# Where 128 w_ada accumulations stand in a one-core diffusion-layer kernel, and decay sums made from high and low parts

## What is computed

```python
sh1, sc1, g1, sh2, sc2, g2 = split(silu(c) @ w_ada + b_ada, 6)   # w_ada: 2048 x 12288
hx = rmsnorm(x) * (1 + sc1) + sh1                                # context: the same with c_ctx
z  = hx @ w_in             # q, k, v, two low-rank columns for decay, g, Hyena inputs, merge gates
la = log_sigmoid(lr @ wg + bg) / 16           # log decay of each direction, 256 x 512
# context: state = sum over tokens of k * exp(b_last - b) and v, with b = cumsum(la)
# latent:  chunked gated linear attention (chunks of 64) in both directions, FFT long convolution
x  = x + g1 * rmsnorm((sigmoid(ga) * (o @ p_gla) + sigmoid(gb) * (y @ p_hy)) @ w_out)
x  = x + g2 * rmsnorm(swiglu(rmsnorm(x) * (1 + sc2) + sh2))
```

## Time and profile before

| | |
|---|---|
| median of 3 runs | 1619.79 us |
| profiled execution, its own time | 1624.13 us |
| span of that execution | 1622.3 us |
| TensorE, busy share of the span | 98% |
| VectorE, ScalarE, GpSimd | 68%, 46%, 5% |
| mean granted TensorE clock | 0.991 |

### The profile page before, as it was taken

How to read it: one execution, slowest core, us unless ns; L and a number is a source line. 1 busy time by engine, 2 the same in 40 slices (tenths; PEclk the granted TensorE clock), 3 DMA queues, 4 the chain that set the end, 5 groups by cost and what they waited for, 6 DMA issues and landing times.

```text
span 1622.3 us, 22565 instructions
## 1 busy us (share of the span) xinstructions
PE 1593.1 (98%) x8540; PEld 1310.5 (81%) x8540; DVE 1102.0 (68%) x1325; ACT 751.6 (46%) x902; POOL 81.6 (5%) x157
## 2 busy tenths in 40 slices
PE   6999999999999999999999999999999999999998
PEld 4656678888888888888788888888888888888886
DVE  5668675788789868778776666666665556555556
ACT  5433225634544434444345545555445554444444
POOL 0011020000000001100100000000000000000000
PEclk9999999999999999999998999999999999999999
DMA  9999877766677768966984777777776656656653
GB/s 343 322 325 357 284 242 217 212 191 195 204 212 236 235 209 281 310 213 213 334 270 169 229 231 237 237 231 237 238 231 200 190 186 206 195 193 194 194 193 118
DMA packets 264785, 377.74 MB, mean 233 GB/s; under 512 B 14177, under 2 KB 223436, under 8 KB 263180
## 3 DMA queue, kind: packets, MB, share of 16 engines
q1 hardware_dynamic: 243008, 297.57, 58.3%
q0 software_dynamic: 20816, 78.91, 14.7%
q10 hardware_dynamic: 892, 0.33, 0.1%
HBM read 372.57 MB, written 4.19 MB: 232 GB/s over the span
## 4 chain that ended last, share of the span: by engine, by line
PE 92%; DMA 3%; DVE 2%; SPq 1%; issue 1%; ACT 0%; DVEq 0%; ACTq 0%
PE ps L1713 39%; PE ps L1720 19%; PE ps L1728 9%; PE ps L1729 8%; PE ps L1730 8%; PE ps L1655 2%; DMA a2raw<-in_w_ada 1%; SPq L438 1%; DMA ada_raw<-in_w_ada 1%; DVE lo L1152 1%; PE ps L1852 1%; PE ps L1864 0%; PE ps L1643 0%; PE ps L1890 0%; PE ps L1815 0%
## 5 line engine op out<-in xcount | busy, mean ns | idle before, releaser
L1484 DVE TENSOR_TENSOR lo<-raw,hi 128x1024 fp32r<-128x1024 f32 x252 | 308.3, 1224 | 245.7 <-ACT hi L920 245.2
L1713 PE MATMUL ps<-hx,hi 128*128 128x512 f32 x1392 | 437.6, 396 | 1.5 <-DVE lo L1484 0.8
L920 ACT ACTIVATE hi<-raw 128x1024 fp32r<-128x1024 f32 x252 | 266.8, 1060 | 313.6 <-PE ps L1720 200.5
L665 ACT ACTIVATE hi<-raw 128x1024 fp32r<-128x1024 f32 x224 | 236.9, 1060 | 296.6 <-PE ps L1720 164.1
L1713 PE MATMUL ps<-hxc,hi 128*128 128x512 f32 x1088 | 347.7, 401 | 0.0
L1720 PEld LDWEIGHTS ps<-hx,lo 128*128 128x128 f32 x1408 | 265.6, 189 | 62.9
L1152 DVE TENSOR_TENSOR lo<-raw,hi 128x1024 fp32r<-128x1024 f32 x224 | 269.1, 1219 | 66.7 <-ACT hi L665 66.5
L1720 PE MATMUL ps<-hx,lo 128*128 128x256 f32 x1408 | 277.6, 279 | 0.0
L1720 PEld LDWEIGHTS ps<-hxc,lo 128*128 128x128 f32 x1088 | 205.4, 189 | 48.6
L1720 PE MATMUL ps<-hxc,lo 128*128 128x256 f32 x1088 | 214.6, 279 | 0.0
L1713 PEld LDWEIGHTS ps<-hx,hi 128*128 128x128 f32 x1392 | 211.9, 189 | 2.4 <-DVE lo L1484 1.0
(11 more groups left out here) (334 smaller groups left out, 1699.6 us busy)
## 6 DMA issues: line engine op xcount, KB each, us to landing
raw<-in_w_in SPq DMA_DIRECT2D x160, 512.0 KB, 4.6
a2raw<-in_w_ada POOLq DMA_DIRECT2D x100, 512.0 KB, 5.1
raw<-in_ffn_gate SPq DMA_DIRECT2D x88, 512.0 KB, 4.5
raw<-in_ffn_up SPq DMA_DIRECT2D x88, 512.0 KB, 4.5
raw<-in_ffn_down SPq DMA_DIRECT2D x88, 512.0 KB, 4.6
ada_raw<-in_w_ada SPq DMA_DIRECT2D x64, 512.0 KB, 9.4
raw<-in_w_out SPq DMA_DIRECT2D x32, 512.0 KB, 5.4
a2k<-in_w_ada POOLq DMA_DIRECT2D x28, 512.0 KB, 5.9
```

The costliest lines, as they stand in the source:

```text
L665: nc.scalar.activation(high_of(uu), raw[:, slot_of(uu), :], ACT.Copy).then_inc(hi_done, 1)
L920: nc.scalar.activation(hi[:, slot, :], raw[:, uu % RING, :], ACT.Copy).then_inc(hi_done, 1)
L1484: V.tensor_tensor(lo[:, uu % RING, :], raw[:, uu % RING, :], hi[:, uu % 4, :].bitcast(f32), SUB).then_inc(lo_done, 1)
L1713: mm(bank(b + t), (hi[:, uu % 4, :] if w_h is None else w_h)[:, c0:c0 + P], feat[:, k, :], start=first, stop=False)
```

## The change

It does five things.

1. `NKS` is 26: two pieces (of chunk 3's second half) move from block 7 to the place where four of that half already stood (now pieces 58 to 63). In blocks 3, 5 and 7 the positions differ: block 3 has 4 pieces instead of 5, block 5 has 5 (position 6 is new), block 7 has 4 and ends at position 6.
2. GpSimd holds back piece 16 (and so 17) until position 7 of block 5 is done.
3. From unit 137 on 18 pieces stand at distances of 1.4 units (before 16 at 1.5), then 5 beside p (before 4), and 15 from unit 201 on at distances of 1.1 units (before 16 from unit 192 at 1.6).
4. x is reloaded in two halves with no pieces between them, behind piece 82 (before behind piece 83, with two pieces between the halves).
5. A step `dcut` splits `lac` and `la` into a float32r high part (ScalarE) and a low part (VectorE); for the context it also copies the five triangles to float32r. `ctxw` and `kstate` use two float32r matmuls for each plain one, with the same triangle. `ctxw`, `ctxs`, `kstate` and `kturn` stand one unit later.

```diff
-        STEPS = [("lrsum", 0, 25, "apd"), ("decay", 1, 27, "pa"), ("dexp", 1, 28, "a"),
-                 ("dln", 1, 29, "ad"), ("ctxw", 0, 32, "pad"), ("ctxs", 0, 35, "pa"),
+                 ("dln", 1, 29, "ad"), ("dcut", 1, 30, "ad"), ("ctxw", 0, 33, "pad"), ("ctxs", 0, 36, "pa"),
                  ("decay", 0, 37, "pa"), ("dexp", 0, 38, "a"), ("dln", 0, 39, "ad"),
-                 ("kstate", 0, 42, "pad"), ("kturn", 0, 44, "pad")]
+                 ("dcut", 0, 40, "ad"), ("kstate", 0, 43, "pad"), ("kturn", 0, 45, "pad")]
...
-        NKS = 28
+        NKS = 26
-        A2_KV = [(), (), (7, 9, 11), (1, 3, 6, 9, 11), (1, 3, 6, 9, 11), (0, 2, 4, 11),
-                 (1, 3, 5, 8, 10), (0, 2, 4, 6, 8, 9)]
+        A2_KV = [(), (), (7, 9, 11), (1, 4, 7, 10), (1, 3, 6, 9, 11), (0, 2, 4, 6, 11),
+                 (1, 3, 5, 8, 10), (0, 2, 4, 6)]
         A2_AT = ([28 + int(2.4 * a) for a in range(19)] + [81, 86, 91, 96, 99, 102, 105, 108, 110, 112, 119, 121, 123]
-                 + [137 + int(1.5 * a) for a in range(16)] + [162, 170, 178, 186]
-                 + [192 + int(1.6 * a) for a in range(16)])
+                 + [137 + int(1.4 * a) for a in range(18)] + [164, 170, 176, 182, 187]
+                 + [201 + int(1.1 * a) for a in range(15)])
...
             for a in range(5, NKS):
+                if a == 16:
+                    pool.wait_ge(kv_pe, 12 * 5 + 8)
                 a2_load(a)
...
-            for a in range(60, 84):
+            for a in range(58, 83):
                 a2_load(a)
             pool.wait_ge(ev_dve, N_GRP["w"][0])
             for t in range(2):
                 pool.dma_start(x1[:, t, :], x[P * t:P * (t + 1), :]).then_inc(s_x1, 16)
-                for a in range(84 + 2 * t, 86 + 2 * t):
-                    a2_load(a)
-            for a in range(88, 96):
+            for a in range(83, 96):
                 a2_load(a)
...
+                elif name == "dcut":                      # ScalarE
+                    if i:
+                        act.wait_ge(s_tri, 16)
+                        nc.scalar.activation(tri_r[:].rearrange("p a n -> p (a n)"),
+                                             cp[:, K_TRI:K_TRI + 5 * P], ACT.Copy)
+                    dst, src = (lac_h, lac) if i else (la_h, la)
+                    nc.scalar.activation(dst[:], src[:], ACT.Copy).then_inc(done, 1)
...
+                elif name == "dcut":                      # VectorE
+                    dst, src, high = (lac_l, lac, lac_h) if i else (la_l, la, la_h)
+                    V.tensor_tensor(dst[:], src[:], high[:].bitcast(f32), SUB).then_inc(done, 1)
...
-                            ins = mm(bank(2 * d + t), tri[d], lac[:, t, cols], start=True,
+                            mm(bank(2 * d + t), tri_r[:, d], lac_h[:, t, cols], start=True,
+                               stop=False)
+                            ins = mm(bank(2 * d + t), tri_r[:, d], lac_l[:, t, cols], start=False,
                                      stop=far is None)
...
-                            ins = mm(bank(2 * d + t), trc[d], la[:, t, 512 * d:512 * (d + 1)],
-                                     start=True, stop=True)
+                            mm(bank(2 * d + t), tri_r[:, 3 + d], la_h[:, t, 512 * d:512 * (d + 1)],
+                               start=True, stop=False)
+                            ins = mm(bank(2 * d + t), tri_r[:, 3 + d],
+                                     la_l[:, t, 512 * d:512 * (d + 1)], start=False, stop=True)
```

More of the change, by code:

```diff
@@ L122, in layer @@
         osq = at("osq", O_RC + 28 * KB, [P, 2, DV])
+        lac_h = at("lac_h", O_RC + 16 * KB, [P, 2, 1024], f32r)
+        lac_l = at("lac_l", O_M + 48 * KB, [P, 2, 1024], f32r)
+        la_h = at("la_h", O_RC + 24 * KB, [P, 2, 1024], f32r)
+        la_l = at("la_l", O_M + 8 * KB, [P, 2, 1024], f32r)
+        tri_r = at("tri_r", O_GB, [P, 5, P], f32r)
         t_a = at("t_a", O_M, [P, 2, 1024])
@@ L350, in a2_part @@
                 return 3, a // 16, a % 16, a2k[:, a % 2, :], acck[:]
-            if 60 <= a < 64:
+            if 58 <= a < 64:
                 return 3, 1, a - 48, a2raw[:, a % 2, :], acck2[:]
-            chunk, r = (2, a - NKS) if a < 60 else (4, a - 64) if a < 96 else (5, a - 96)
+            chunk, r = (2, a - NKS) if a < 58 else (4, a - 64) if a < 96 else (5, a - 96)
             half = r % 2
@@ L553, in _ @@
             pool.wait_ge(kv_ev, 12 * (NB - 1))
-            for a in range(NKS, 49):
+            for a in range(NKS, 47):
                 a2_load(a)
@@ L561, in _ @@
             pool.dma_start(kk2[:, :, :, 0:512], kk4[:, :, :, 0:512]).then_inc(s_kkl[0], 16)
-            a2_load(49)
+            a2_load(47)
             pool.dma_start(kk2[:, :, :, 512:HY], kk4[:, :, :, 512:HY]).then_inc(s_kkl[1], 16)
-            a2_load(50)
+            a2_load(48)
             pool.dma_start(inv[:], k_inv.rearrange("k p n -> p k n")).then_inc(s_inv, 16)
-            for a in range(51, 57):
+            for a in range(49, 55):
                 a2_load(a)
@@ L569, in _ @@
             pool.dma_start(grow[:], b_ada[:, 2 * D:3 * D].broadcast_to([P, D])).then_inc(s_row[0], 16)
-            for a in range(57, 60):
+            for a in range(55, 58):
                 a2_load(a)
@@ L1077, in a2 @@
                     dve.wait_ge(kv_ev, 12 * (NB - 1))
-                elif a in (60, 64, 65):
+                elif a in (58, 64, 65):
                     dve.wait_ge(x_sem["d"], upto(STEPS, "d", stepno("row")))
@@ L1081, in a2 @@
                     dve.wait_ge(j_cols, 1)
-                if k == 0 or a == 60:
+                if k == 0 or a == 58:
                     V.tensor_scalar(dst, src, cs[:, 0, k:k + 1], None, MUL).then_inc(a2_done, 1)
@@ L1788, in step @@
                 elif name == "red":
-                    pe.wait_ge(a2_done, 60)
+                    pe.wait_ge(a2_done, 58)
                     for q in range(4):
@@ L1804, in step @@
                             cols = slice(512 * d, 512 * (d + 1))
-                            ins = mm(bank(2 * d + t), tri[d], lac[:, t, cols], start=True,
+                            mm(bank(2 * d + t), tri_r[:, d], lac_h[:, t, cols], start=True,
+                               stop=False)
+                            ins = mm(bank(2 * d + t), tri_r[:, d], lac_l[:, t, cols], start=False,
                                      stop=far is None)
                             if far is not None:
-                                ins = mm(bank(2 * d + t), tri[2], lac[:, far, cols], start=False,
-                                         stop=True)
+                                mm(bank(2 * d + t), tri_r[:, 2], lac_h[:, far, cols], start=False,
+                                   stop=False)
+                                ins = mm(bank(2 * d + t), tri_r[:, 2], lac_l[:, far, cols],
+                                         start=False, stop=True)
                 elif name == "ctxs":
```

## The result

The changed kernel takes 1626.07 us (median of 10 runs, 1622.78 to 1630.48). Beside it on the same chip the kernel before takes 1620.82 (10 runs, 1618.59 to 1627.31). The ratio is 1.0027, with a 95% interval of 1.0016 to 1.0038: 0.27% slower, 5.2 us by the medians. In size that is within the 0.3% that I called the limit of a measurement, but the interval leaves no change out. The predicted 1614.5 us and the range 1607 to 1622 both miss.

The account below looks back on a forecast made before the run. TensorE, busy 98% of the span, was taken to bound the kernel. Terms -5.3 + 1.2 - 3.8 + 1.7 = -6.2 us gave 1617.9 from the profiled 1624.1, 1613.6 from the runs' median; forecast 1614.5, range 1607 to 1622.

Parts of the forecast that it names:

- part 1: Beside keys and values, 26 instead of 28 accumulations: the last one's wait and the clock fall behind it go, -5.3 us.
- part 2: Block 5 of keys and values: the piece moved to position 6 lands late, +1.2 us; holding transfers back costs nothing.
- part 3: Decay's sums: float32r matmuls replace half-rate passes, 4.0 us less TensorE work, net gain 3.8 us.
- part 4: w_out: x without pieces between its halves gains 1.8 us, the crowded list costs 3.5; net cost 1.7 us.
- (a): w_out: pieces of w_ada set the pace, costing 7.7 us instead of 3.5, total 1618.7 us; chance 0.18.
- (c): w_out: transfers, not TensorE, set the unit once landings exceed about 7 us; 1627 us or more; chance 0.14.
- (b): Block 5: piece 15 lands late, TensorE idles 3.4 us more, with a longer half-clock stretch; 1618.4 us; chance 0.14.

## Why the prediction was wrong, step by step

I cut each trace into stretches between ends of matmul groups, and count a stretch at half clock apart (half its length is lost; where TensorE idles within one, half of that idle time lands in this column too, so the split between the two columns is rough and their sum is not). Each term is then a difference between the mean of the traces that have an edit and the mean of those that don't.

| term | predicted | measured: waits and work | half clock | sum |
|---|---|---|---|---|
| part 1, 26 pieces | -5.3 | -1.2, and +0.7 for a late piece in block 7 | -2.3 | -2.8 |
| part 2, block 5 | +1.2 | +1.3 | +3.0 | +4.3 |
| part 3, split sums | -3.8 | -3.0 | 0 | -3.0 |
| part 4, w_out | +1.7 | +4.8 | +2.4 | +7.2 |
| sum | -6.2 | +2.6 | +3.1 | +5.7 |

The sum stands near the medians' +5.2. It leaves out one stretch: behind w_out TensorE runs at half clock in every trace, and loses 5.1 us there in the seven traces of the changed kernel and its variants with two buffers, 6.8 in the three made from the kernel before, and 6.8 and 3.4 in the two with three buffers. For the changed kernel that takes 1.7 back, and the sum would be +4.0; nothing in the change was meant to touch this stretch, and why it differs is open. The other lists of part 4 (18 pieces from unit 137 on, five beside p) cost nothing, as forecast: from 310 us to the end of p all twelve traces agree within 0.1 us. No run has part 1 by itself; its row rests on comparing nine traces with 26 pieces and three with 28.

Two steps make 8.6 of the 11.9 us between forecast and result. In both I named the wait that came and sized it too short, and in both I put the half clock behind the new waits at nothing, without a reason, although part 1 charges that very thing. By the table's columns the clock is 5.4 of the 8.6.

**Part 4 was mis-sized: 7.2 us for 1.7.** The sum took the median landing of 6.1 us and 0.1 us of handing over, 3.74 us a piece. In the stretch that set the pace the landings took 6.5 us in the median, up to 7.0, and the handing over 0.3: (6.58 + 1.28 + 0.30) / 2 = 4.08. That is 1.36 us more than a unit for each piece, not 1.02, and it holds as long as VectorE waits at each landing, as it did for seven pieces in a row. The median of 5.8 from 800 to 832 hides this, because the last three of its pieces landed in 3.8 to 4.6 us, when 219 GB/s were moved (window from 820) and not 320. It is the pace of rival (a), 3.94 us at a landing of 6.5; its net of -1.8 + 7.7 = 5.9 us stands beside 4.8 measured without the clock and 7.2 with it. I had charged no clock there: behind the waits of the timeline above a stretch ran at half clock (0.85 in the window from 820), 2.4 us lost in the mean. Right was the gain of 1.8 us from x in one go (full windows from 790 to 810). The waits came somewhat early: before units 208 to 211, where I had put them at 211 and 217. Rival (c), transfers as the limit, is refuted by the third buffer: landings of 6.8 us and no idle time. From the end of the first group of three matmuls of unit 192 to the end of unit 223 (half clock taken off) it is 88.5 us in the two traces with the old list and x, 93.3 in five with the changed ones and 86.4 in both with three buffers. So the kernel before already lost 2.1, and the changed one waits 6.9 where I had added up 3.5.

The Trainium skill (DMA: Bandwidth & Descriptors, Where 436 GB/s comes from), cited above for 358 GB/s as a core's limit for reads, does not hold for such a window: with three buffers this case moved 401 and 398 GB/s in 10 us. Where page and measurement differ, the measurement decides.

**Part 2 was mis-sized: 4.3 us for 1.2.** The piece was asked for at 169.82, as worked out (169.8), but took 7.7 us where I had taken the 7.2 us median and then 1.5 off, for one piece less in the queue. That subtraction had no row behind it, and no trace shows such a gain: with 28 pieces and the same place the piece came as late (177.79). VectorE waited 3.24 us, not 0.9, the reduction came at 179.39, 3.9 us later and not 2.2, and TensorE idled 2.1 us more, not 1.2. The step also left out the clock: in the seven traces with the piece at position 6 the mean loss in block 5 is 4.4 us, in five without it 1.4. Counted with idle time kept apart, the seven idle 2.1 us more and lose 2.2 more to the clock. This is rival (b): it put 5.1 us on this step (1.2 + 3.9). The kernel with this move alone is slower by 0.33%. The hold at nothing was right.

**Part 1 was right for its execution, less for the mean.** The idle time and the fall at 232 are gone, as I said. But I charged what one execution showed: it idled 1.86 us and lost 3.4 at half clock, where the two other traces with 28 pieces idled 0.92 and 0.52 and lost 1.7 each. The new last piece, at position 6 of block 7, was late itself in some traces (0.71 us at 226.13): I had called its transfer early because it ran at that place before.

**Part 3 was 0.8 us too good.** Work fell by 2.1 + 1.6 = 3.7 us (the first matmul took longer); the wait was 0.69 us and not 0.2, since I counted the copy of the triangles as ScalarE's work but not as standing in the way of the other copy.

In size the result falls among the times within 0.3% of before, on which 0.37 stood, but by neither the sum nor the range that I gave. The joint error is that I gave (a) and (b) 0.18 and 0.14 as if only one could come. Both did, they come from the same fact (two buffers and a long landing), and together they give 1614.5 + 4.2 + 3.9 = 1622.6, already at the edge of the range.

Open is what sets the length of a half-clock stretch: in the traces with the piece at position 6 the windows from 180 to 190 have a clock between 0.55 and 0.83. Not tried was the copy of the triangles moved ahead of the wait, worth 0.7 us at most.

## What to carry to other kernels

With n buffers a stream can't be faster than one item each (landing + wait for its user + use) / n; compare this with the distance at which the items are used, and take the landing at the load of that stage, no better. Where a list is crowded, try a third buffer before another distance. In this case a large transfer (x, 2 MB) could go ahead of the small ones only where the next of them was due some 15 us or more behind its request: next pieces landed 14.0 and 15.4 us behind it in the lists from 192 and 196. And an idle wait of 2 us on the engine that bounds the kernel is to be charged at about twice its length, since the clock can fall behind it (here 7.3 us of waits in block 5, w_out and block 7's end went with 7.7 us of half clock; not behind every wait, as 790 to 800 in the earlier trace rows shows).

## What was not expected of the hardware

- Half-clock stretches follow the same waits but are not the same length: by the granted clock of each run (its missing share times the span), the kernel before loses 12.6 us on average (19 runs) and the changed one beside it 15.7 (6 runs). The kernel with the old places and three buffers loses 9.7. With this loss taken off, the changed kernel is 1.8 us slower than the one before; with it, 4.9. In its first ten runs it lost 13.7, so this share is not well known.
- A piece of 512 KB took 3.8 to 7.0 us to land in the changed kernel's w_out (6.5 where pieces are crowded), 7.7 in block 5, and 12.9 and 13.6 behind two transfers of 1 MB on the same queue.
- A float32r matmul of 512 columns takes 0.23 us in the chain, but the first behind a wait of 0.69 us stands there with 0.50 (262.53).
